# Streamed activations of a fused two-block network begin at a place of their own in each stage

## What is computed

```python
def swiglu(h, w_gate, w_up, w_down):
    return (jax.nn.silu(h @ w_gate) * (h @ w_up)) @ w_down
...
h = modulate(x, norm_g[i, 0], mod[:, 0, 0], mod[:, 0, 1])
x = x + FFN_RES_WEIGHT * mod[:, 0, 2][:, None, :] * swiglu(
    h, ffn_w_gate[i, 0], ffn_w_up[i, 0], ffn_w_down[i, 0])
...
    act = jax.nn.gelu(jnp.einsum('td,ted->te', hx, u_sel), approximate=False)
    return jnp.einsum('te,ted->td', gx * act, v_sel)
```

## Time and profile before

| | us |
|---|---|
| median of 2 runs | 3401.72 |
| the two runs | 3394.63, 3408.81 |
| the profiled execution | 3391.88 |
| its span, first to last instruction | 3390.0 |
| mean granted TensorE clock | 0.987 of full speed |

### The profile page before, as it was taken

How to read it: one execution, slowest core, us unless ns; L and a number is a source line. 1 busy time by engine, 2 the same in 40 slices (tenths; PEclk the granted TensorE clock), 3 DMA queues, 4 the chain that set the end, 5 groups by cost and what they waited for, 6 DMA issues and landing times.

```text
span 3390.0 us, 68787 instructions
## 1 busy us (share of the span) xinstructions
PE 3251.1 (96%) x26804; PEld 3108.9 (92%) x26804; DVE 2581.1 (76%) x4576; ACT 1608.2 (47%) x2594; POOL 196.5 (6%) x331
## 2 busy tenths in 40 slices
PE   6999989999999998999999999998899999999998
PEld 5999769999867997989999999998789999999998
DVE  7989667989836997747978777776846978877777
ACT  3466644454445445144455444445325445544444
POOL 1100001111100111200000000000300000000000
PEclk8999999999999999999999999999999999999999
DMA  9964218979603973045755477774114665567775
GB/s 373 385 225 166 73 50 337 391 283 387 269 20 124 397 299 130 7 162 189 235 199 177 169 240 237 231 233 159 63 67 167 234 221 183 172 211 234 232 234 184
DMA packets 246578, 707.46 MB, mean 209 GB/s; under 512 B 27472, under 2 KB 93008, under 8 KB 244928
## 3 DMA queue, kind: packets, MB, share of 16 engines
q1 hardware_dynamic: 212112, 571.64, 48.4%
q0 software_dynamic: 34224, 132.46, 10.1%
HBM read 669.40 MB, written 34.60 MB: 208 GB/s over the span
## 4 chain that ended last, share of the span: by engine, by line
PE 81%; DMA 7%; DVE 6%; ACT 3%; issue 2%; SPq 0%; POOL 0%; DVEq 0%; ACTq 0%
PE psum L514 34%; PE psum L547 27%; DMA ring<-stream 6%; PE psum L1071 3%; PE psum L893 2%; PE psum L1006 1%; PE psum L644 1%; DVE ring L1638 1%; PE psum L913 1%; PE psum L495 1%; ACT weights_hi L1143 1%; PE psum L526 1%; PE psum L527 1%; DVE arena L1696 1%; PE psum L728 1%
## 5 line engine op out<-in xcount | busy, mean ns | idle before, releaser
L514 PE MATMUL psum<-hh,weights_hi 128*128 128x256 f32 x4216 | 1189.2, 282 | 24.5 <-DVE ring L1638 12.0
L1143 ACT ACTIVATE weights_hi<-ring 128x1024 fp32r<-128x1024 f32 x711 | 752.7, 1059 | 955.7 <-DMA ring<-stream 895.6
L1638 DVE TENSOR_TENSOR ring<-ring,weights_hi 128x1024 fp32r<-128x1024 f32 x711 | 870.2, 1226 | 409.5 <-ACT weights_hi L1143 404.6
L514 PE MATMUL psum<-h,weights_hi 128*128 128x256 f32 x4216 | 1172.2, 278 | 0.0
L514 PE MATMUL psum<-hh,ring 128*128 128x256 f32 x2976 | 829.0, 279 | 0.0
L514 PEld LDWEIGHTS psum<-hh,weights_hi 128*128 128x128 f32 x4216 | 796.6, 189 | 34.3 <-DVE ring L1638 17.2
L514 PEld LDWEIGHTS psum<-h,weights_hi 128*128 128x128 f32 x4216 | 798.7, 189 | 0.3
L547 PE MATMUL psum<-small,weights_hi 128*128 128x256 f32 x2752 | 768.8, 279 | 2.6 <-DVE ring L1638 1.6
L547 PE MATMUL psum<-work,weights_hi 128*128 128x256 f32 x2752 | 765.9, 278 | 0.0
L547 PE MATMUL psum<-small,ring 128*128 128x256 f32 x2304 | 642.2, 279 | 0.0
L514 PEld LDWEIGHTS psum<-hh,ring 128*128 128x128 f32 x2976 | 563.3, 189 | 0.0
(11 more groups left out here) (410 smaller groups left out, 3894.0 us busy)
## 6 DMA issues: line engine op xcount, KB each, us to landing
ring<-stream SPq DMA_DIRECT2D x735, 512.0 KB, 3.9
arena<-mod_weights POOLq DMA_DIRECT2D x224, 512.0 KB, 7.0
arena<-stream SPq DMA_DIRECT2D x222, 512.0 KB, 6.4
acts<-small SPq DMA_DIRECT2D x256, 128.0 KB, 2.2
work<-acts SPq DMA_DIRECT2D x256, 128.0 KB, 3.0
arena<-cond_rows POOLq DMA_DIRECT2D x3, 1024.0 KB, 7.1
arena<-w_uq POOLq DMA_DIRECT2D x1, 3072.0 KB, 10.6
arena<-constants POOLq DMA_DIRECT2D x2, 1200.0 KB, 5.7
```

Source lines behind the costliest of these rows:

```text
L514: mm = pe.matmul(out, lhs[:, d, :], rhs[:, d, :], start=(d == 0 and p == 0), stop=(d == DT - 1 and p == 2))
L1143: act.activation(whi[:, NTH[n] % WS, :], raw(n), ACT.Copy).then_inc(sem["block_hi"], 1)
L1638: dve.tensor_tensor(low(n), raw(n), whi[:, NTH[n] % WS, :].bitcast(F32), ALU.subtract)\
```

## The change

The activations get two larger tiles. `h_and_hh` holds both parts of the normed activations and 128 values to spare, `work_and_small` both parts of the gated ones with the work space and 32 values to spare. In each stage the streamed tiles begin `H_AT[s]` or `G_AT[s]` values (4 bytes each) behind the start of their region, the rounded part and the rest alike. `zeros` now stands between the two, and `ahead_of_activations` is gone. All other uses of the memory are at the start of their region as before, `rs` and `rv` 32 values later.

Added up with starts at multiples of 32 bytes, `h_and_hh` begins at 800 modulo 1024 and `work_and_small` at 544. The distance of a streamed tile from the start of a weight tile, modulo 512 bytes, is 448 before in all stages, and then:

| stage | 0 | 1 | 2 | 3 | 4 | 5 | 6 | 7 | 8 | 9 |
|---|---|---|---|---|---|---|---|---|---|---|
| normed activations | 168 | 232 | 296 | 360 | 328 | 392 | 408 | 456 | 472 | 488 |
| gated activations | 424 | | 440 | 472 | | 504 | | 424 | | 24 |

Modulo 1024 these distances are 680 to 1000 and 424 to 536. (The 400 to 976 of a short description are the same places if sizes are added up without rounding to 32 bytes.) Each new place lies 8 bytes behind a multiple of 16; each old one is a multiple of 32. No instruction, wait or DMA is added or taken away, and none is moved.

```diff
+H_AT = (2, 18, 34, 50, 42, 58, 62, 74, 78, 82)
+G_AT = {0: 2, 2: 6, 3: 14, 5: 22, 7: 2, 9: 30}
+LATEST_H, LATEST_G = 128, 32
...
-        zeros = sb("zeros", [P, P], BF16)
         eps = sb("eps", [P, 20])
         modc = sb("modc", [P, NSUB, 24])
         omk = sb("one_minus_k_a", [P, 8])
-        sb("ahead_of_activations", [P, 2])
-        h, (h_lo,) = sb_twice("h", [P, DT, T], [([P, DT, T], F32R)])
-        hh, (h_hi,) = sb_twice("hh", [P, DT, T], [([P, DT, T], F32R)])
-        work, (_, gat_lo) = sb_twice("work", [P, 2048], [([P, 1024], F32), ([P, 4, T], F32R)])
-
-        small, (gat_hi, _) = sb_twice("small", [P, 5, T], [([P, 4, T], F32R), ([P, T], F32)])
-
-        ijg, rs, rv = small[:, 0:3, :], small[:, 3, :], small[:, 4, :]
+        n_h, n_g = 2 * DT * T + LATEST_H, 2048 + 5 * T + LATEST_G
+        h_all, (h_round,) = sb_twice("h_and_hh", [P, n_h], [([P, n_h], F32R)])
+        zeros = sb("zeros", [P, P], BF16)
+        work_all, (work_round,) = sb_twice("work_and_small", [P, n_g], [([P, n_g], F32R)])
+
+        def tiles(whole, at, n):
+
+            return whole[:, at:at + n * T].rearrange("p (a t) -> p a t", t=T)
+
+        def h_of(s):
+            return tiles(h_all, H_AT[s], DT)
+
+        def h_lo_of(s):
+            return tiles(h_round, H_AT[s], DT)
+
+        def h_hi_of(s):
+            return tiles(h_round, DT * T + H_AT[s], DT)
+
+        def gat_of(s):
+            return tiles(work_all, 1024 + G_AT[s], 4)
+
+        def gat_lo_of(s):
+            return tiles(work_round, 1024 + G_AT[s], 4)
+
+        def gat_hi_of(s):
+            return tiles(work_round, 2048 + G_AT[s], 4)
+
+        h, hh = tiles(h_all, 0, DT), tiles(h_all, DT * T, DT)
+        work, ijg = work_all[:, 0:2048], tiles(work_all, 2048, 3)
+        rs, rv = (work_all[:, 2048 + LATEST_G + i * T:2048 + LATEST_G + (i + 1) * T] for i in (3, 4))
...
-            def columns_in_parts(out, w, wl):
-
+            def columns_in_parts(s, out, w, wl):
+
+                h_hi, h_lo = h_hi_of(s), h_lo_of(s)
                 for d in range(DT):
                     for p, (lhs, rhs) in enumerate(((w, h_hi), (w, h_lo), (wl, h_hi))):
...
-                    rows_in_parts(w, wl, gat_hi[:, k, :], gat_lo[:, k, :], last)
+                    rows_in_parts(w, wl, gat_hi_of(7 + 2 * l)[:, k, :], gat_lo_of(7 + 2 * l)[:, k, :], last)
...
-                dve.tensor_tensor(gat[:, k % 4, :], sil[:, k % 4, :], WALL[:, :, i * 4 + k], ALU.mult).then_inc(sem["pe_gated"], 1)
+                dve.tensor_tensor(gat_of(7 + 2 * l)[:, k % 4, :], sil[:, k % 4, :], WALL[:, :, i * 4 + k], ALU.mult).then_inc(sem["pe_gated"], 1)
```

More of the change, by code:

```diff
@@ L309, in build @@
         sil = work[:, 0:1024].rearrange("p (b t) -> p b t", b=4)
-        gat = work[:, 1024:2048].rearrange("p (b t) -> p b t", b=4)
         SQ = AR[:, 120:128, :]
@@ L373, in build @@
         MB = flat(h[:, 0:6, :]).rearrange("p (a b) -> p a b", a=2)
-        SFR, OHB = gat_lo[:, 0, :], gat_lo[:, 1, 0:64]
+        SFR, OHB = work_round[:, 1024:1024 + T], work_round[:, 1024 + T:1024 + T + 64]
         ARG_BANKS = (4, 5, 3, 1)
@@ L559, in ffn @@
                         w, wl = parts(base + 2 * k + half_)
-                        columns_in_parts(PS[:, k % 2, half_ * T:(half_ + 1) * T], w, wl)
+                        columns_in_parts(s, PS[:, k % 2, half_ * T:(half_ + 1) * T], w, wl)
                 for j in range(FT):
@@ L563, in ffn @@
                     pe.wait_ge(sem["gate_lo"], GATES["ffn", f] + j + 1)
-                    rows_in_parts(w, wl, gat_hi[:, j % 2, :], gat_lo[:, j % 4, :], j == FT - 1)
+                    rows_in_parts(w, wl, gat_hi_of(s)[:, j % 2, :], gat_lo_of(s)[:, j % 4, :], j == FT - 1)
             def out_project(first, rhs, ktiles=8):
@@ L593, in ssd @@
                             pe.wait_ge(sem["conv_step"], 4 * SSD_X.index(p - 4) + 4)
-                    columns_in_parts(PS[:, p % 4, 0:T], w, wl)
+                    columns_in_parts(1, PS[:, p % 4, 0:T], w, wl)
                     if p == 20:
@@ L702, in mla @@
                         pe.wait_ge(sem["proj_evac"], ev + p - 3)
-                    columns_in_parts(PS[:, p % 4, 0:T], w, wl)
+                    columns_in_parts(4, PS[:, p % 4, 0:T], w, wl)
                 pe.wait_ge(sem["mla_w"], 64)
@@ L819, in rwkv @@
                     pe.wait_ge(sem["proj_evac"], EV["mix_in", l] + p - 1 + PRIME)
-                    columns_in_parts(PS[:, p % 2, 0:T], w, wl)
+                    columns_in_parts(6 + 2 * l, PS[:, p % 2, 0:T], w, wl)
                     if p == L + 2:
@@ L1039, in peer @@
                         pe.wait_ge(sem["proj_evac"], EV["peer_q", l] + n - 3 + PRIME)
-                    columns_in_parts(PS[:, n % 4, 0:T], w, wl)
+                    columns_in_parts(7 + 2 * l, PS[:, n % 4, 0:T], w, wl)
                 pe.wait_ge(sem["proj_evac"], EV["peer_q", l] + 16 + PRIME)
@@ L1133, in shift @@
                     act.wait_ge(sem["norm_scaled"], 8 * s + d + 1)
-                    to = h_hi if s in IN_PARTS else h
-                    act.activation(to[:, d, :], h[:, d, :], ACT.Identity, bias=modc[:, s, d:d + 1], scale=1.0)\
+                    act.activation(h_hi_of(s)[:, d, :], h_of(s)[:, d, :], ACT.Identity, bias=modc[:, s, d:d + 1], scale=1.0)\
                        .then_inc(sem["h_ready"], 1)
@@ L1155, in gate_hi @@
                     act.wait_ge(sem["ffn_a"], FT * f + j + 1)
-                    act.activation(gat_hi[:, j % 2, :], ATF[:, j, :], ACT.Copy).then_inc(sem["gate_hi"], 1)
+                    act.activation(gat_hi_of((0, 2, 3, 5)[f])[:, j % 2, :], ATF[:, j, :], ACT.Copy).then_inc(sem["gate_hi"], 1)
                 split_hi(base + 3)
@@ L1472, in gate_hi @@
                     act.wait_ge(sem["block_used"], i * 4 + (v0 + k - 3))
-                    act.activation(gat_hi[:, k % 4, :], gat[:, k % 4, :], ACT.Copy).then_inc(sem["gate_hi"], 1)
+                    act.activation(gat_hi_of(7 + 2 * l)[:, k % 4, :], gat_of(7 + 2 * l)[:, k % 4, :], ACT.Copy).then_inc(sem["gate_hi"], 1)
                 for n in range(NK):
@@ L1613, in normed @@
                     g = modc[:, s, 8 + d:9 + d] if s < NSUB else col("lnf", d)
-                    dve.scalar_tensor_tensor(h[:, d, :], x[:, d, :], g, rs[:, :], ALU.mult, ALU.mult)\
+                    to = h_of(s) if s < NSUB else h
+                    dve.scalar_tensor_tensor(to[:, d, :], x[:, d, :], g, rs[:, :], ALU.mult, ALU.mult)\
                        .then_inc(sem["norm_scaled" if s < NSUB else "out_ready"], 1)
@@ L1644, in rest_of_h @@
                     dve.wait_ge(sem["h_ready"], 8 * s + d + 1)
-                    dve.scalar_tensor_tensor(h_lo[:, d, :], h[:, d, :], modc[:, s, d:d + 1], h_hi[:, d, :].bitcast(F32), ALU.add,
+                    dve.scalar_tensor_tensor(h_lo_of(s)[:, d, :], h_of(s)[:, d, :], modc[:, s, d:d + 1], h_hi_of(s)[:, d, :].bitcast(F32), ALU.add,
                                              ALU.subtract).then_inc(sem["h_lo"], 1)
@@ L1661, in gate_lo @@
                     dve.wait_ge(sem["gate_hi"], GATES["ffn", f] + j + 1)
-                    dve.tensor_tensor(gat_lo[:, j % 4, :], ATF[:, j, :], gat_hi[:, j % 2, :].bitcast(F32), ALU.subtract)\
+                    dve.tensor_tensor(gat_lo_of(s)[:, j % 4, :], ATF[:, j, :], gat_hi_of(s)[:, j % 2, :].bitcast(F32), ALU.subtract)\
                        .then_inc(sem["gate_lo"], 1)
@@ L2108, in gated @@
                         dve.wait_ge(sem["block_used"], i * 4 + (v0 + k - 3))
-                    dve.tensor_tensor(gat[:, k % 4, :], sil[:, k % 4, :], WALL[:, :, i * 4 + k], ALU.mult).then_inc(sem["pe_gated"], 1)
+                    dve.tensor_tensor(gat_of(7 + 2 * l)[:, k % 4, :], sil[:, k % 4, :], WALL[:, :, i * 4 + k], ALU.mult).then_inc(sem["pe_gated"], 1)
                 def gate_lo(k, i):
                     dve.wait_ge(sem["gate_hi"], i * 4 + (GATES["uv", l] + k + 1))
-                    dve.tensor_tensor(gat_lo[:, k % 4, :], gat[:, k % 4, :], gat_hi[:, k % 4, :].bitcast(F32), ALU.subtract)\
+                    dve.tensor_tensor(gat_lo_of(7 + 2 * l)[:, k % 4, :], gat_of(7 + 2 * l)[:, k % 4, :],
+                                      gat_hi_of(7 + 2 * l)[:, k % 4, :].bitcast(F32), ALU.subtract)\
                        .then_inc(sem["gate_lo"], 1)
```

## The result

The changed kernel takes 3480.65 us (median of 2 runs, 3478.36 and 3482.95) against 3401.72: ratio 1.0232, interval 1.0136 to 1.0328. It is slower by 79 us; whether by more than 2%, two runs a side don't tell.

A forecast was written before the change was run, and what follows sets the result against it. TensorE's streamed matmuls were taken to bound the kernel; 3391.9 - 19 = 3373 from the profiled execution and 3401.7 - 25 = 3377 from a median one gave 3375 us predicted, range 3345 to 3425.

The forecast's parts named there:

- What bounds the kernel: Whole kernel: TensorE, busy 96% of the span, paced by 21,624 matmuls of one shape on L514 and L547.
- the three levels: Matmul steps: 0.1133 and 0.1178 us, both on L514 and L547 at the same addresses, and 0.1198 us on L811.
- the 28 us of excess: Matmuls at 0.1178 instead of 0.1133 us: 23 us in nine long stretches of stages 7 and 9, 5 in shorter pieces.
- the cover: Claim that nothing hides the 28 us: VectorE busy 22.65 of 30 us, ScalarE 15.00, so others keep up with 0.1133.
- moving the one against the other makes the bad timing rarer: Streamed tile's reads moved against the weights' reads, mostly in stages 7 and 9: two thirds of the excess goes, -19 us.
- the level of L811: L811, streaming at distance 0 from the weights, steps by 0.1198 us; all 21,624 matmuls there: bound of +113 us.
- within 40 bytes of the old 448: Stages 7 and 9: new distances 456, 424 and 488 lie this near the old one, at which both 0.1133 and 0.1178 occur.
- The other side: Rival, all streamed tiles: new places, 8 bytes off a multiple of 16, are worse; at most 3461 us; chance 0.24.
- stages 0 to 5 leaving 8.82 matmuls per us: Sign in the new profile that the new places are worse in themselves; 8.82 is the rate of 0.1133 us steps.
- The milder form: Stages 5 and 9: 7056 matmuls within 24 bytes of distance 0 go at L811's step, 46 us more; 3423 us.
- the place doesn't decide: Rival, all streamed matmuls: waits, not places, throw TensorE into 0.1178; time of before, 3392 to 3402 us; chance 0.25.
- The lower floor: Rival, L514 and L547: 0.1133 itself sinks to 0.1116 us, 37 us more saved, 3327 us; chance 0.08.

The follow-up runs named there:

- the map: Kernel without the networks, only triples of matmuls, streamed tile at 64 distances from the weights, 0 to 504 bytes in steps of 8; 113.3 to 122.2 ns per matmul.
- 256 pairs: Part of a second matmul-only kernel: rounded part and rest at places of their own, 16 x 16 distances in steps of 16 bytes; no step below 113.3 ns.

## Why the prediction was wrong

**What bounds the kernel, and the three levels: right.** The counts over stretches, the levels of 0.1133, 0.1178 and 0.1198 and the 28 us of excess stood (29 from all starts). So did the cover: VectorE's and ScalarE's times didn't move, and no other engine took over.

**The step that failed** is "moving the one against the other makes the bad timing rarer ... two thirds of the excess goes, -19 us". In its place stood +118 us of slower steps, 31 of them hidden, most of these in shorter waits: +87. I had a bound for it, all matmuls at the level of L811 (+113), and took it for remote; the steps reached it. Two things were wrong in that. First, I took nearness in bytes for nearness in behaviour ("within 40 bytes of the old 448"). The map has nothing of the kind: 448 has 113.3, 440 and 456 have 120, and the aligned 432 and 464 have 119. Second, I read L811's level as the price of distance 0 alone. It is the common one: of 32 distances in steps of 8 bytes 30 are above 116 ns once settled, and 448 was one of the two exceptions. With three levels at two places the rows couldn't tell which place was the exception, and I assumed that it was the slow one. The range from 3345 to 3425 followed from that and missed by 56 us; it should have reached to the bound.

**The other side** was named, with its mechanism, tiles 8 bytes off a multiple of 16, and with its sign, stages 0 to 5 leaving 8.82 matmuls per us, which came true. The changed kernel, the one with 8 bytes at the old distance and the map bear it out. It is half of the cause: with the same places 8 bytes earlier, all aligned, the loss was still 44 of the 82 us by which the changed kernel lies above the 3398.60 of before in that comparison, and that part is the distance's. Its price was wrong too: I put such a stream into the upper level at most, 3461 us, while it goes to 0.120. By the Trainium skill ("SBUF — State Buffer", Specifications), which has lines of 16 bytes, the new places would be slower, and they are; one line more on 64, an estimate from that page, would be 1.6%. Averaged over the map, 8 bytes more cost 2.1%; from the good place 448 they cost 5.9%. That it is the line which costs, no run shows. The milder form, nearness to distance 0 in stages 5 and 9, isn't what happened: their gated tiles step by 0.1198 and 0.1200, but so do those of stage 0 at 424.

**That the place doesn't decide** is refuted by the changed kernel, by the 8 bytes at the old distance and by the map. The rule cited for it, the Trainium skill's two independent read ports ("TensorE: Matmul & The Clock Gate", Part 2), doesn't give the time here: with nothing else on the core, the place alone moves the step from 113.3 to 122.2 ns, and weights moved by 8 bytes under an unmoved stream move it from 113.3 to 118.3. Whether the loads take something from the streams, or either is slow by itself, stays open, since no run streams without loading. **The lower floor** wasn't found either: 113.3 is the least of 64 distances and 256 pairs. L893, from which I took 0.1116, multiplies plain float32 and not float32r, so it was no measure of that floor.

**What stays open**: why the step depends on the place with a period of 256 bytes; whether it is the distance from the weights or the streamed tile's own place that counts; and which waits throw TensorE into the upper level, since in the full kernel some of up to 1.3 us do and others as long don't.

## What to carry to other kernels

If TensorE paces a kernel with float32r, the place of the streamed tile is worth a few per cent, and it has to be measured: one small kernel with nothing but the matmuls of one shape maps all places in a single run, and here its numbers held for most stages of the full kernel to half a nanosecond. Map with the weights where the full kernel has them. Keep every streamed tile on a multiple of 16 bytes, counted with the allocator's own rounding; that isn't enough, so give one good distance to all stages, and the same one to the rounded part and the rest. Where a count over stretches shows two levels at one address, time the kernel often, and look for a place that has but one level.

## What the runs showed of the hardware

- The step of matmuls with 128x128 float32r weights and 256 float32r columns takes 113.3 to 122.2 ns at full clock, by the distance between the streamed tile and the weights modulo 256 bytes, for weights that begin at 128 modulo 256; 112 and 192 are the two good ones, and streams 4 or 8 bytes off a multiple of 16 take 117.8 to 122.2. With weights 8 bytes further, six streams took 118.3 to 123.7.
- Distance 192 has a second state of 117.8 ns that holds over more than 100 us of matmuls. Of 20 waits that cost 24 to 149 ns nine set it off, of 43 that cost 158 to 438 ns none did; in the full kernel waits of up to 1.3 us came before it. Distance 112 didn't show it in two full kernels and 64 bursts.
- With half the columns in each matmul, and in plain float32, L893 still steps by 111.6 ns.
